# Order of the input projections around a gated scan: forget slots third and fourth, the scan's values beside its first steps

## The chip, the cores and the metric

One core of one Trainium2 chip (trn2). The metric is the device time of one execution in microseconds. TensorE (PE), VectorE (DVE), ScalarE (ACT), Pool (GpSimd) and the DMA queues run their own instruction streams and meet at semaphores. Weights are streamed from HBM by the queue of SyncE (SP).

## The reference

Two layers over 512 latent and 256 context tokens of width 1024. In each layer the input, scaled and shifted by a modulation of the conditioning vector, goes through one combined projection that is cut into fourteen column groups:

```
(qa, ka, va, qb, kb, vb, qc, ic, fcf, fcb, gc, qd, kd, vd) = _split_cols(px)
```

Four head groups use them: A windowed attention, B attention with normalised and rotated queries and keys, C a gated linear recurrence in both directions (HGRN2), D neighbourhood attention. For C, qc are the queries, ic the values, fcf and fcb the logits of the forget gates forward and backward, gc the output gate. The gate is f = lb + (1 - lb) * sigmoid(z), the key 1 - f, and the state is carried over chunks, context tokens first, then latent tokens, once in each direction. The four outputs are concatenated and projected, followed by a gated residual with layer norm, a convolutional feed-forward of width 2816 and a second residual. The context tokens are dropped after layer 0.

## The kernel before

All products are float32 made of three fp32r products (high by high, low by high, high by low), so every weight is split into a high and a low half: ScalarE writes the high half (`high_weights`, L1398), Pool the low half (`low_weights`, L2415).

The projection is done in twelve slots of 256 columns: QA, KVA, QB, KVB, QC, IC, FCF, FCB, GC, QD, KD, VD. A slot is worked off in parts: `tok` parts of two token tiles (L945), or `feat` parts of 128 features over the latent or the context tokens (L939). A part has four pieces, which `project` issues.

`ORDERS` gives the order of the slots in each layer. `mixer_jobs(l)` cuts it in two: the own stage, worked off before the scan, and the parts beside the scan, whose pieces are dealt out to the scan's units. In layer 0 the own stage also holds 21 modulation products (`mod`, L850), numbers 8 to 28, which are dealt out between the parts; each reads one weight slot of 1 MB.

The scan (`hgrn`) has 24 units per layer: forward 12 and backward 12, each direction two context tiles and four latent tiles, two head pairs per tile. In layer 1 the context units (0 to 3 and 12 to 15) have no output and only carry the state. For a unit Pool prepares the gate (`YB`, `KB`, L2381 to L2384), ScalarE takes the logarithm (L1508), VectorE scans it (L2012) and subtracts references (L2022), ScalarE takes exponentials (L1532 to L1538), VectorE forms the queries and keys (L2033, L2047), TensorE makes the score maps (L1081) or only turns the keys (L1088), VectorE copies them under a mask (L2089), and TensorE makes the output and the state (L1104 to L1115). TensorE's queue is: maps of unit i, the first piece of the unit, outputs of unit i - 1, the rest of the pieces.

After each projection part ScalarE copies the sum out of PSUM (`take_projections`). VectorE then does, in order of the parts: for a forget part `forget` (add, reciprocal, scale: L1990 to L1992), for QB and KVB `square_heads` (L1871 to L1882) and, after Pool's root (`head_roots`, L2345), `rotate` (L1901 to L1938), for QA and KVA `rotate` alone. VectorE enters the scan only when it has done this for the whole own stage. A rotation is held back by one part (`pending`), and beside the scan by one unit (`waiting`). Pool, too, takes the roots of the own stage before the first gate preparation.

Weights go through a ring of places (`ring_plan`). SP issues the loads in the order of their first use (`STREAM`), each when the slot that held the place has been used; a load that waits holds up those behind it. Places 0 to 2 are `WR`, place 3 is `U[:, 3072:5120]`, open to the first 29 modulation slots. The gates of FCB are written to `U[:, 3072:4608]` (`cz[1]`), those of FCF to `U[:, 4608:6144]` (`cz[0]`). The rule takes the free place whose slot has its last use first:

```
place = min(free, key=lambda p: -1 if holder[p] is None else final[STREAM[holder[p]]])
```

Before, layer 0's own stage was QC, GC, IC, QB, KVB, FCF, with FCB beside units -2 and -1; layer 1's was QC, GC, IC and the context half of FCF, with the rest of FCF beside units -2 and -1 and FCB beside units 0 to 3.

Of the kernel before, what the change touches and what calls it, by code (L numbers as in the profile page):

```python
# [4 lines left out]

# [1 line left out]
D_MODEL, SEQ, CTX, DEPTH = 1024, 512, 256, 2  # L7
# [3 lines left out]
NLT, NCT = SEQ // P, CTX // P  # L11
# [16 lines left out]
RING = 3  # L28
# [7 lines left out]
QA, KVA, QB, KVB, QC, IC, FCF, FCB, GC, QD, KD, VD = range(12)  # L36
# [10 lines left out]
def slot_parts(l, s):  # L47
# [4 lines left out]
    if s in FEATURE:  # L52
# [1 line left out]
    return [("tok", p, 0) for p in range(2 + ctx)]  # L54


ORDERS = ((QC, GC, IC, QB, KVB, FCF, FCB, QA, KVA, VD, QD, KD),
          (QC, GC, IC, FCF, FCB, QA, KVA, QB, KVB, VD, QD, KD))
PIECES = 4
UNITS = 4 * NT  # L60


def mixer_jobs(l):

    whole = lambda s: [(("in", l, s, 0), p) for p in slot_parts(l, s)]
    order = ORDERS[l]
    gate = order.index(FCF)
    own = [p for s in order[:gate] for p in whole(s)]
    if l == 0:
        own = own[:2] + own[4:6] + own[2:4] + own[6:]  # L70
    forget = whole(FCF)
    extra = [(("mod", n // 24, n % 24, 0), ("mod", n, 0)) for n in range(MOD_FIRST, 24 + EARLY)] if l == 0 else []
    mixed, n = own[:1], len(own) - 1
    for k, part in enumerate(own[1:]):
        mixed += [part] + extra[k * len(extra) // n:(k + 1) * len(extra) // n]
    if gate == 3:
        mixed += forget[:2]
        early, flow = forget[2:], [p for s in order[gate + 1:] for p in whole(s)]
    else:
        mixed += forget  # L80
        early, flow = whole(FCB), [p for s in order[gate + 2:] for p in whole(s)]
    span = lambda p: 5.8 if p[0] == "tok" else 2.9 if p[2] else 5.45
    total = sum(span(p) for _, p in flow)
    jobs, at = [], 0.0
    for i, (key, part) in enumerate(early):
        jobs.append((key, part, [2 * i // len(early) - 2] * PIECES))
    for key, part in flow:
        steps = [at + span(part) * q / PIECES for q in range(PIECES)]
        jobs.append((key, part, [int(t / total * (UNITS + 1)) for t in steps]))
        at += span(part)  # L90
    return mixed, jobs


def weight_splits(l):
# [62 lines left out]
def ring_plan():  # L157

    final = {key: n for n, key in enumerate(USES)}
    places = RING + 1 + ENTRANCE + 1  # L160
    holder, count, plan = [None] * places, [0] * places, []
    for n, key in enumerate(STREAM):
        kind, l = key[:2]
        first = kind == "mod" and (l == 0 or key[2] < EARLY)
        inner = kind in ("up", "down") or l > 0 and (kind == "mod" and not first or key in (("in", l, QC, 0), ("in", l, GC, 0)))
        free = range(1 if inner else 0, RING + 1 if first else RING)
        if kind == "mod" and l == 0 and key[2] < MOD_FIRST:
            free = range(SPARE - 1, 0, -1)
        if kind in ("up", "down") and l == DEPTH - 1 or kind == "mod" and l > 0 and key[2] >= LATE:
            free = (SPARE,) + tuple(free)  # L170
        place = min(free, key=lambda p: -1 if holder[p] is None else final[STREAM[holder[p]]])
        count[place] += 1
        plan.append((place, count[place], holder[place]))
        holder[place] = n
    return plan
# [6 lines left out]
def hybrid_backbone(nc, weights, x, ctx_in, consts, masks, params, bias_d, ln_rows, kept, vrows, out):  # L182
# [14 lines left out]
    with stack:  # L197
# [35 lines left out]
        whole = lambda e: (e[:, 0:2 * TOK], e[:, 2 * TOK:ENTRY])  # L233
# [173 lines left out]
        job_act = sem("job_act")  # L407
# [69 lines left out]
        jobs = []  # L477
        for l in range(DEPTH):
            own, late = mixer_jobs(l)
# [51 lines left out]
        for l in range(DEPTH):  # L531
            for d in range(2):
                order = [NLT + c for c in range(NCT)][::1 - 2 * d] + list(range(NLT))[::1 - 2 * d]
# [13 lines left out]
        beside, pieces_at = {}, {}  # L547
# [40 lines left out]
        for l in range(DEPTH):  # L588
            au = atts_of[l]
            first = n_chunk  # L590
# [99 lines left out]
        for m, (l, i) in enumerate(res):  # L690
            total = FT if i else KT
# [148 lines left out]
        def _(pe):  # L840
# [223 lines left out]
            def hgrn(l):  # L1064
# [54 lines left out]
                for i in range(len(us) + 1):  # L1119
                    if i < len(us):  # L1120
                        u = us[i]
                        pe.wait_ge(ke, u.g + 1)
                        if i >= 2:
                            if us[i - 2].out:
                                pe.wait_ge(atd, us[i - 2].no + 1)
                            if us[i - 2].state:
                                pe.wait_ge(kd_in, us[i - 2].ns + 1)
                        if u.out:
                            score_maps(u)
                        if u.state:  # L1130
                            turn_keys(u)
                    here = pieces_at[l, i]
                    ahead = int(1 <= i < len(us) and len(here) >= 2)
                    for j, q in here[:ahead]:
                        project(l, j, q)
                    if i >= 1:
                        outputs(us[i - 1])
                    for j, q in here[ahead:]:
                        project(l, j, q)
# [579 lines left out]
        def _(dve):  # L1719
            steps = [0]  # L1720
# [236 lines left out]
            def project(l):  # L1957
                pending = []
# [5 lines left out]
                for j in own_of[l]:  # L1964
# [12 lines left out]
                    if j.slot == GC:  # L1977
                        dve.wait_ge(job_act, j.after[0])
                        for i in range(2):
                            g = cg[:, 2 * j.a + i, :]  # L1980
                            dve.tensor_tensor(g, g, onorm[:, l, :], ALU.mult)
                assert not pending

            def forget(j):
                lo, hi = (0, SEQ) if j.b == 0 else (SEQ, TOK)
# [651 lines left out]
```

## Time and profile before

| | |
|---|---|
| median of 3 runs | 1959.86 us (1958.93 to 1963.39) |
| profiled execution | 1959.74 us, its span 1957.9 us |
| mean granted clock of TensorE | 0.984 |
| TensorE matmul / weight load | 1865.0 us / 1583.4 us |
| VectorE, ScalarE, Pool | 1307.4, 889.0, 929.8 us |
| DMA | 179.38 MB, mean 92 GB/s |
| layer 0: own stage, scan | about 57 to 180 us, 180 to 385 us |
| layer 1: own stage, scan | about 1177 to 1215 us, 1215 to 1426 us |

The profile is of one execution. Busy times are those of the engine's own instructions; an engine that waits is idle. The granted clock is the share of full speed that TensorE was given in a stretch: 1.00 is 2.4 GHz, 0.5 is 1.2 GHz, a mean between them says for how much of the stretch it was at the lower one.

### The profile page before, as it was taken

The numbers are of one execution on the slowest core, as the hardware profiler recorded it, in microseconds if no ns is written. First come the engines' busy times: TensorE is split into PE (matmuls) and PEld (weight loads), VectorE is DVE, ScalarE is ACT, GpSimd is POOL, SyncE is SP. The second block draws the span as 40 slices with busy tenths as digits, with TensorE's granted clock in tenths as the row PEclk, the third lists the DMA queues.
The fourth block names the chain that finished last, engine by engine and source line by source line (L and its number), as shares of the span: only waits on it lengthen the run. The fifth ranks groups of instructions, "written<-read, shape, count | busy, mean of one in ns | idle before, by whom it ended". The sixth has DMA issues, their size and how long they took to land.

```text
span 1957.9 us, 32562 instructions
## 1 busy us (share of the span) xinstructions
PE 1865.0 (95%) x12406; PEld 1583.4 (81%) x12406; DVE 1307.4 (67%) x2506; ACT 889.0 (45%) x1909; POOL 929.8 (47%) x770
## 2 busy tenths in 40 slices
PE   6899799999999999999999999998999989999997
PEld 4788798867778888888888878898877778888886
DVE  4238999676684977978735263998776858247545
ACT  3224688577533222222343343665567443333542
POOL 3135567121435344554453344666432545765743
PEclk8999899999999999999999999999999999999999
DMA  8563101220111322333222121101130313223321
GB/s 356 216 221 124 41 27 34 74 84 2 44 65 44 130 99 95 108 108 108 87 76 86 54 87 65 66 31 42 50 135 2 130 43 129 105 89 140 119 107 44
DMA packets 29545, 179.38 MB, mean 92 GB/s; under 512 B 3024, under 2 KB 6224, under 8 KB 10320
## 3 DMA queue, kind: packets, MB, share of 16 engines
q1 hardware_dynamic: 26720, 169.18, 23.8%
q10 hardware_dynamic: 2672, 8.13, 1.1%
q8 instruction: 100, 1.64, 0.3%
q14 instruction: 53, 0.43, 0.1%
HBM read 172.05 MB, written 5.24 MB: 91 GB/s over the span
## 4 chain that ended last, share of the span: by engine, by line
PE 70%; DVE 19%; issue 4%; ACT 3%; DMA 2%; POOL 2%; DVEq 0%; SPq 0%; ACTq 0%; POOLq 0%
PE PS L1342 22%; PE PS L1237 19%; PE PS L945 8%; PE PS L939 5%; DVE W L1756 4%; PE PS L1199 3%; PE PS L1175 3%; PE PS L1081 2%; PE PS L1159 2%; DMA WR<-in_weights 2%; DVE W L1754 1%; DVE U L1991 1%; PE PS L1293 1%; PE PS L1165 1%; PE PS L850 1%
## 5 line engine op out<-in xcount | busy, mean ns | idle before, releaser
L1342 PE MATMUL PS<-XH,WS 128*128 128x512 f32 x2016 | 540.3, 355 | 0.9 <-POOL WS L2482 0.9
L1342 PEld LDWEIGHTS PS<-XH,WS 128*128 128x128 f32 x2016 | 358.1, 189 | 54.4 <-POOL WS L2482 1.3
L1342 PE MATMUL PS<-XL,WS 128*128 128x512 f32 x1008 | 356.9, 354 | 0.0
L2482 POOL TENSOR_TENSOR WS<-WR,WS 128x1024 fp32r<-128x1024 f32 x78 | 189.8, 2433 | 260.0 <-ACT WS L1624 260.0
L1692 ACT ACTIVATE W<-PS,PR 128x768 f32<-128x768 f32 (+1 forms) x88 | 78.0, 886 | 416.6 <-PE PS L1342 354.4
L1342 PEld LDWEIGHTS PS<-XL,WS 128*128 128x128 f32 x1008 | 190.7, 189 | 26.3
L2304 DVE SCALAR_TENSOR_TENSOR W<-PS,PR,W 128x511 f32<-128x511 f32 (+1 forms) x132 | 82.9, 656 | 179.7 <-ACT W L1692 179.7
L2415 POOL TENSOR_TENSOR WL<-WR,EU 128x512 fp32r<-128x512 f32 x96 | 131.0, 1392 | 131.1 <-ACT EU L1398 131.1
L945 PE MATMUL PS<-EU,XH 128*128 128x256 f32 x624 | 186.8, 300 | 5.8 <-issue 5.5
L945 PE MATMUL PS<-WL,XH 128*128 128x256 f32 x624 | 179.0, 288 | 0.0
L945 PE MATMUL PS<-EU,HL 128*128 128x256 f32 x624 | 177.2, 288 | 0.0
L945 PEld LDWEIGHTS PS<-EU,XH 128*128 128x128 f32 x624 | 122.6, 197 | 13.6 <-issue 10.7
L1756 DVE SCALAR_TENSOR_TENSOR W<-WR,SC,W 128x256 f32<-128x256 f32 x210 | 130.2, 661 | 3.7
L945 PEld LDWEIGHTS PS<-WL,XH 128*128 128x128 f32 x624 | 122.9, 197 | 0.0
L945 PEld LDWEIGHTS PS<-EU,HL 128*128 128x128 f32 x624 | 121.7, 197 | 0.1
L2442 POOL COPY W<-ST 128x256 f32<-128x256 f32 x30 | 15.0, 500 | 197.9 <-DVE ST L2143 197.9
L1237 PE MATMUL PS<-XH 128*128 128x512 f32 x450 | 107.8, 390 | 0.0
L1237 PE MATMUL PS<-EW 128*128 128x512 f32 x450 | 106.5, 390 | 0.2 <-DVE W L2309 0.2
L939 PE MATMUL PS<-XH,EU 128*128 128x512 f32 (+1 forms) x288 | 102.1, 366 | 3.5 <-ACT XH L1406 3.5
L1237 PE MATMUL PS<-XL 128*128 128x512 f32 x420 | 100.1, 389 | 0.0
L1237 PE MATMUL PS<-EU 128*128 128x512 f32 x420 | 99.3, 390 | 0.0
L1237 PEld LDWEIGHTS PS<-EW 128*128 128x128 f32 x450 | 84.2, 188 | 18.1 <-DVE W L2309 0.8
(231 smaller groups left out, 4264.8 us busy)
## 6 DMA issues: line engine op xcount, KB each, us to landing
WR<-in_weights SPq DMA_DIRECT2D x115, 1024.0 KB, 4.8
U<-in_weights SPq DMA_DIRECT2D x16, 1024.0 KB, 7.6
H<-in_weights SPq DMA_DIRECT2D x13, 1024.0 KB, 4.8
H<-in_x SPq DMA_DIRECT2D x2, 2048.0 KB, 11.6
U<-in_bias SPq DMA_DIRECT2D x2, 1792.0 KB, 9.8
H<-in_ctx SPq DMA_DIRECT2D x2, 1024.0 KB, 16.1
U<-in_ln_rows ACTq DMA_DIRECT2D x2, 1024.0 KB, 5.4
WR<-in_weights SPq DMA_DIRECT2D x4, 512.0 KB, 3.6
```

Source lines behind the costliest of these rows:

```text
L939: return pe.matmul(bank(j.bank, CTX if j.b else SEQ), w[:, j.a * P:(j.a + 1) * P], acts, start=start, stop=stop)
L945: return pe.matmul(bank(j.bank)[:, i * 256:(i + 1) * 256], acts, w, start=start, stop=stop)
L1081: mm = pe.matmul(maps_of(u, hh)[:, m * 64:(m + 1) * 64], KE[par][rows, m, :], later(QL[par][rows, m, :], u, w), start=True, stop=True)
L1175: mm = pe.transpose(tb[:, (b - c.lo) * P:(b - c.lo + 1) * P], PB[c.a.r % 2][:, b * P:(b + 1) * P], ident)
L1199: mm = pe.matmul(bank(7)[64 * hh:64 * hh + 64, a.p * P:(a.p + 1) * P], vv[a.grp][:, kt, vc:vc + 64], PT[a.r % 2][:, b * P:(b + 1) * P], st ...
L1237: mm = pe.matmul(bank((job + 4) % 8), acts[a][:, t * P:(t + 1) * P], rows[b], start=(q.k == 0 and n == 0), stop=(q.k == total - 1 and n == 2))
L1342: mm = pe.matmul(PS[u.pos][:, lo:hi], w[:, part, k, :], src[:, k, lo:hi], start=(k == 0 and src is xh3 and part == 0), stop=(k == KT - 1 a ...
L1692: act.activation(dst[:, 0:n], PS[u.pos][:, 0:n], ACT.Identity, bias=convp[:, l, 3, jj:jj + 1], scale=convp[:, l, 1, jj:jj + 1]).then_inc(b ...
L1756: ins = dve.scalar_tensor_tensor(acc, wk[:, k, :], scv[:, k, v:v + 1], acc, ALU.mult, ALU.add)
L2304: ins = dve.scalar_tensor_tensor(y[:, lo + 1:hi], ps[:, lo:hi - 1], convp[:, l, 0, jj:jj + 1], y[:, lo + 1:hi], ALU.mult, ALU.add)
L2415: pool.tensor_tensor(raw_piece(WL, l, at, q), raw_piece(WR, l, at, q), high_piece(l, at, q), ALU.subtract).then_inc(in_low, 1)
L2482: pool.tensor_tensor(ws5[:, u.c % 2, 1], half_slot(u), ws5[:, u.c % 2, 0], ALU.subtract).then_inc(w_low, 1)
```

## The change

In both layers the slots FCF and FCB come third and fourth, and all of FCF and FCB belongs to the own stage. IC follows beside units -2 and -1. In layer 0 the rest of the order is as before; in layer 1 the order beside the scan is QB, QA, KVA, KVB, VD, QD, KD. The pieces beside layer 1's scan are dealt out by a share: 1.75 for a unit without output (0 to 3 and 12 to 15), 1 for the others. Place 3 of the ring is open only to modulation slots that are used before FCF in layer 0. TensorE waits for ScalarE's copies of IC before the outputs of unit 0, and VectorE does the last held-back rotation at the end of its own stage.

```diff
-ORDERS = ((QC, GC, IC, QB, KVB, FCF, FCB, QA, KVA, VD, QD, KD),
-          (QC, GC, IC, FCF, FCB, QA, KVA, QB, KVB, VD, QD, KD))
+ORDERS = ((QC, GC, FCF, FCB, QB, KVB, IC, QA, KVA, VD, QD, KD),
+          (QC, GC, FCF, FCB, IC, QB, QA, KVA, KVB, VD, QD, KD))
...
-    gate = order.index(FCF)
+    gate = order.index(IC)
     own = [p for s in order[:gate] for p in whole(s)]
     if l == 0:
         own = own[:2] + own[4:6] + own[2:4] + own[6:]
-    forget = whole(FCF)
+    early, flow = whole(IC), [p for s in order[gate + 1:] for p in whole(s)]
     extra = [(("mod", n // 24, n % 24, 0), ("mod", n, 0)) for n in range(MOD_FIRST, 24 + EARLY)] if l == 0 else []
-    mixed, n = own[:1], len(own) - 1
+    mixed, n = own[:1], len(own) - 2
     for k, part in enumerate(own[1:]):
         mixed += [part] + extra[k * len(extra) // n:(k + 1) * len(extra) // n]
-    if gate == 3:
-        mixed += forget[:2]
-        early, flow = forget[2:], [p for s in order[gate + 1:] for p in whole(s)]
-    else:
-        mixed += forget
-        early, flow = whole(FCB), [p for s in order[gate + 2:] for p in whole(s)]
     span = lambda p: 5.8 if p[0] == "tok" else 2.9 if p[2] else 5.45
     total = sum(span(p) for _, p in flow)
+    share = [1.75 if l + 1 == DEPTH and i % (UNITS // 2) < 2 * NCT and i < UNITS else 1.0 for i in range(UNITS + 1)]
+    ends = [e / sum(share) * total for e in itertools.accumulate(share)]
...
-        jobs.append((key, part, [int(t / total * (UNITS + 1)) for t in steps]))
+        jobs.append((key, part, [sum(e <= t + 1e-6 for e in ends) for t in steps]))
...
+def ahead_of_gates():
+
+    own = [key for key, _ in mixer_jobs(0)[0]]
+    return own[:own.index(("in", 0, FCF, 0))]
...
+    opening = ahead_of_gates()
...
-        free = range(1 if inner else 0, RING + 1 if first else RING)
+        free = range(1 if inner else 0, RING + 1 if first and key in opening else RING)
...
+                    if i == 1:
+                        pe.wait_ge(job_act, beside[l, -1][-1].after[0])
...
-                assert not pending
+                if pending:
+                    rotate(pending.pop())
```

## Rows read from the trace of the kernel before

**Rows 1.** The page: busy time of each engine.

```profile
PE 1865.0 (95%) x12406; PEld 1583.4 (81%) x12406; DVE 1307.4 (67%) x2506; ACT 889.0 (45%) x1909; POOL 929.8 (47%) x770
```

**Rows 2.** Windows: length; busy (count) of PE, PEld, DVE, ACT, POOL; clock, DMA share, GB/s.

```profile
57.00:90.00 33.00, 27.02 (x251) 22.02 (x244) 9.35 (x33) 10.50 (x25) 7.25 (x7) 0.90 0.60 224
90.00:182.00 92.00, 91.87 (x824) 80.78 (x823) 47.74 (x139) 27.23 (x57) 35.21 (x36) 1.00 0.55 198
...
196.30:225.50 29.20, 19.98 (x186) 19.25 (x186) 28.68 (x45) 15.34 (x51) 12.51 (x19) 0.82 0.11 38
225.50:300.00 74.50, 71.12 (x747) 68.62 (x745) 73.29 (x190) 59.04 (x190) 49.99 (x69) 1.00 0.10 34
...
1209.00:1252.80 43.80, 40.86 (x235) 35.20 (x233) 36.21 (x45) 23.52 (x63) 30.22 (x44) 0.96 0.21 73
1252.80:1320.70 67.90, 65.34 (x657) 63.42 (x656) 63.21 (x147) 44.10 (x139) 43.81 (x56) 1.00 0.10 34
1320.70:1354.70 34.00, 26.62 (x195) 25.38 (x194) 30.29 (x84) 17.01 (x52) 23.96 (x32) 0.90 0.17 60
```

**Rows 3.** TensorE's waits, from 57 to 90, 182 to 400 and 1209 to 1430.

```profile
PE PS L850 <- DMA U<-in_weights: 4.9, 1, 4.9
...
PE PS L1081 <- DVE W L2047: 12.3, 6, 7.6
...
PE PS L1088 <- DVE W L2047: 5.1, 2, 3.9
...
PE PS L945 <- issue: 2.8, 1, 2.8
```

**Rows 4.** The chain that ended last, layer 0's own stage: start, length, what.

```profile
70.91 3.09 PE PS L939 x24
...
74.01 7.41 DMA WR<-in_weights
...
81.56 1.94 PE PS L850 x16
83.50 6.43 PE PS L945 x48
...
168.46 5.49 PE PS L939 x24
```

**Rows 5.** DMA issues from 121 to 129.7: count, KB, time to landing.

```profile
WR<-in_weights SPq DMA_DIRECT2D x1, 1024.0 KB, 4.8
U<-in_weights SPq DMA_DIRECT2D x1, 1024.0 KB, 7.2
```

**Rows 6.** VectorE, groups of 182 to 218, then its timeline there.

```profile
L1991 DVE RECIPROCAL U<-U 128x512 f32<-128x512 f32 (+1 forms) x5 | 13.6, 2713 | 0.2
...
L1992 DVE TENSOR_SCALAR U<-U,SC 128x512 f32<-128x512 f32 (+1 forms) x5 | 3.6, 714 | 0.2
...
185.66 1.50 DVE L2012 TENSOR_TENSOR_SCAN W<-W 128x128 f32<-128x128 f32 x1
...
192.89 1.09 DVE L2033 TENSOR_TENSOR W<-W,U 128x896 f32<-128x896 f32 x1 [2.50 <-ACT W L1538]
```

**Rows 7.** The last KVB part in the chain, and Pool's root after it.

```profile
153.18 5.95 PE PS L945 x48
...
164.08 1.36 POOL L2345 TENSOR_TENSOR ST<-ST,SC 128x2 f32<-128x2 f32 x2 [4.85 <-DVE ST L1879]
```

**Rows 8.** VectorE: reciprocals of 1209 to 1262.2; rotations, layers 1 and 0.

```profile
L1991 DVE RECIPROCAL U<-U 128x256 f32<-128x256 f32 (+1 forms) x8 | 20.4, 2553 | 0.3
...
1324.02 0.85 DVE L1901 TENSOR_TENSOR U<-U,ST 128x256 f32<-128x256 f32 x2
...
1329.62 0.76 DVE L1938 TENSOR_TENSOR U<-U 128x256 f32<-128x256 f32 x2
...
1275.94 2.64 DVE L1932 TENSOR_TENSOR U<-U,CN 128x128 f32<-128x128 f32 x2
...
244.57 0.49 DVE L1932 TENSOR_TENSOR U<-U,CN 128x128 f32<-128x128 f32 x2
```

More of the change, by code:

```diff
@@ L2 @@
 from concourse import mybir
+import itertools
 from contextlib import ExitStack
```

## The prediction

> **What bounds the kernel now.** I read the page first: TensorE is busy for 95% of the span [rows 1], so a reordering can only give back TensorE's idle time and the time it runs at the lower clock. Then I cut both layers into stretches, reading TensorE's busy time, VectorE's busy time and the granted clock [rows 2], and asked in each stretch what TensorE waited for [rows 3].
>
> Layer 0. From 57 to 90 us TensorE is idle for 6.0 us at a mean clock of 0.90: weight loads are late. From 90 to 182 us it is idle for 0.1 us. From 196.3 to 225.5 it is idle for 9.2 us at clock 0.82, with VectorE busy for 28.7 of 29.2 us; the longest single wait is one of 7.6 us of the score maps for VectorE [rows 3]. From 225.5 to 300 VectorE is busy 98% and TensorE 95%: the two run almost even.
> Layer 1. From 1209 to 1252.8 TensorE is idle 2.9 us, to 1320.7 (units 4 to 11, the forward units with outputs) 2.6 us with VectorE at 93%, and to 1354.7 (units 12 to 15, no outputs) 7.4 us at clock 0.90.
> So about 12 us of layer 1 and 16 us of layer 0 are idle time, a few more are half clock, and both engines sit near their limit elsewhere.
>
> **The change, layer 0, up to the scan.** The order goes from IC, QB, KVB, FCF to FCF, FCB, QB, KVB, and IC moves beside units -2 and -1, where FCB was. Nothing is added or taken out: IC is three parts of 5.95 us [rows 7], 17.85 us, and FCB two of 5.5 and two of 3.1 [rows 4], less the overlap of one part with the next an estimated 16.8 us. The own stage is thus 1.05 us shorter and the scan's start 1.05 us longer.
> The ring is where it costs. Place 3 lies in U at 3072 to 5119, which is where the gates of FCB and FCF begin. Once they are written early, only what is used before FCF may go there. I walked the planner's rule over the new order: FCF sits in place 1, FCB in place 2, and the modulation slots 13 to 17 all follow each other in place 0; then 18 to 28 all follow each other in place 1. Before, they alternated between two places. A load can only be issued when the slot before it in that place is used, so each modulation product waits for a whole load less the projection that lies between.
> Prices: a lone load lands after 4.8 us; the second of two issued 1.2 us apart after 7.2 [rows 5] (7.4 in [rows 4]); a modulation product takes 1.0 (half of the 1.94 at the low clock), a long part 5.5 to 5.95, a context part 3.1 [rows 4, 7].
> Walking it: slot 12 (behind a 3.1 us part) waits 1.5; slot 14, its load second behind FCB's, 7.2 - 3.1 - 0.25 = 3.85; slot 15 behind a context part 1.5; slot 16 and 17 nothing; slot 18 comes right after 17 and takes the place of FCF: 4.8 - 1.2 = 3.6; slots 19 and 20 1.6 each; 21, 22 nothing; 23, second behind KVB's load, 0.9; 26, second behind IC's, 0.3; 28, directly behind 27 in the same place, 4.8 + 0.1 = 4.9. Sum 19.75. The old waits of this stage go: 4.9 for slot 13, whose issue was held on SP's queue behind IC's (74.01, 7.41 us for slot 14 behind it [rows 4]), and 1.1 for others, in all 6.0 [rows 2, 3], and 3.0 of low clock after the long one (the products of slots 13 and 14 at half pace, 1.94 for one, and 6.43 for a part that takes 5.95 [rows 4, 7], with the start of the load behind them). Slot 12's new 1.5 stands in their place. Net 19.75 - 9.0 - 1.05 = +9.7; I take 8.1, because 1.6 of these waits fall where the clock drop below stretches the projection in front of them.
> The clock: the rows show it at its lower level (1.2 of 2.4 GHz) after idle times of 4.9 and 7.6 us (mean 0.90 and 0.82 over their stretches [rows 2, 3]). The new waits of 3.85, 3.6 and 4.9 are of that size. The last has nothing behind it to absorb it, 3.0; the first two feed the next wait and cost an estimated 0.7 together: +3.7. Bounds 0 and 9.
> So the own stage ends at about 179.7 + 11.8 = 191.5.
>
> **The scan's start.** Removed from VectorE: four forgets of FCB after units -2 to 0. Their reciprocals are 13.6 less FCF's last 3.35, 10.2 us, and with the two scalar instructions around each (0.71 mean for the second, some 0.4 for the first [rows 6]) 13.9. All lay on the path: this is the stretch with VectorE at 98%. The cover that they find is the own stage, where VectorE is busy 47.7 of 92 us [rows 2].
> Added in front: KVB is now the last own part, so its square, Pool's root (1.36 us, [rows 7]) and Pool's first gate preparation come after it, and VectorE's pending rotation. By the rows the root ended 6.3 after TensorE's last product of that part (159.1 to 165.4 [rows 7]); with two modulation sums ahead of it 0.8 more, the preparation and a logarithm 2.6: the first scan starts at 9.7 after the stage's end, where it was 6.0 (185.66 against 179.7 [rows 6]). ScalarE takes both IC parts before the first exponentials, which ends them 2.1 later than the 7.2 they took (185.66 to 192.89). VectorE's path: 11.8 + 3.7 + 2.1 - 13.9 = +3.7. TensorE's path: after IC's 18 us it waits about 3 us for the first maps, then reaches unit 2 at 34.2 after the stage's end; before, 38.4 and 3.7 lost to the clock. 11.8 - 7.9 = +3.9, less some 3 of the later waits for VectorE, which now has a lead. Layer 0: +3.5. The added wait of TensorE for IC's copies stands at unit 1, behind it the outputs of unit 0; the copies are 10 us old by then: 0.
>
> **Layer 1.** FCF and FCB go first; eight forgets (reciprocals 20.4 us, with their neighbours 31 [rows 8]) begin under the own stage at 1193 and end at about 1230. The ring is not touched: no load of place 3 there. TensorE's order becomes IC until 1242.4, then QB over units 0 and 1, QA over 1 to 3, by the share of 1.75. Units 0 to 3 and 12 to 15 get 5.8 to 7.25 us of projection, units 4 to 11 get 26.1 where they had 39.2. QA's low parts (four of Pool's 1.4 us) are split one unit ahead: a wait of about 1 us in place of today's 2.8 [rows 3].
> VectorE decides units 4 to 11. From 1209 to 1320.7 it is busy 36.2 + 63.2 = 99.4 us [rows 2]; less 31 of forgets 68.4. QB's two square-and-rotate groups now come before unit 12: from 1324.02 to 1330.38 one rotation is 6.4 us [rows 8], with the square 7.9, twice 15.8, and KVB's first square 1.3: 85.5. Some 4 of it can be done before QB's first part lands at 1249, VectorE takes it up at 1252.9 and waits 3 for the state sums: 1252.9 + 81.5 + 3 = 1337. TensorE alone could be at unit 12 at 1324. From there before took 34.0 + 71.3; less 8.9 of projections already done, 7.4 of idle time, 3.0 of low clock, plus 1 for small waits: 87.0, end 1424.0 against 1426.1. Layer 1: -2.1. Bounds: 13 less when VectorE does not bind, 8 more when its work all meets Pool's.
> Here the trace shows the same kind of rotation instruction at two prices: 2.64 us for two beside Pool's work and 0.49 alone in layer 0 [rows 8]; I took the mixed sums. The Trainium skill (GPSIMD Engine Reference, Specifications) says that GpSimd's SBUF interfaces are shared with VectorE where VectorE has two SBUF inputs. By that rule alone every rotation beside a split pays the high price and layer 1 ends at +4; the mixed rows give -2.
> Another sentence by itself: the Trainium skill (DMA: Bandwidth & Descriptors, Anatomy of one DMA) puts a load at about 2.0 us and its bytes at 436 GB/s, 4.4 us for a megabyte; by it the six lone waits shrink by 0.4 each and the time would be some 2.4 us lower, while the rows say 4.8.
>
> **Sum.** +3.5 - 2.1 = +1.4 us. The profiled execution took 1959.74 us with a span of 1957.9; the median shown is 1959.86. 1961.3 predicted, span 1959.3. A difference under 0.2% (3.9 us) is about what this kernel's measurement can't tell from none.
>
> **Rivals.**
> 1. The clock falls after most of the new waits of layer 0, also the 1.5 us ones. For: the waits come every 4 to 6 us from slot 14 to 20. Against: waits of this length during the scans leave the mean clock at 1.00 [rows 2]. Price 5 more: 1966.5. It ends slower; it decides from 2.5 us of extra half clock. Chance 0.22.
> 2. VectorE does not bind units 4 to 11: its lead from the early forgets and fewer collisions with Pool let it keep up. For: TensorE then has 13 us less to do there, and units 12 to 15 lose their 7.4 us. Against: the 85.5 us above. Half of the 13 us: 1961.3 - 8 = 1953.5. Faster. Chance 0.32.
> 3. The change does not do what it says in layer 0: the first scan waits for KVB's chain and ScalarE's copies, and the 13.9 us are only waited for elsewhere, TensorE idle again at the first maps with a clock drop. Price 6 to 8: 1968.5. Chance 0.13.
> Forecast, no measurable change, 0.33; its own range 1957 to 1964.
> Range for 8 in 10: 1950, a little beyond rival 2, to 1970, beyond rival 3. Faster 0.32, same 0.33, slower 0.35.
>
> **What would show it.** TensorE idle in the own stage of layer 0 with weight loads as releaser, six or more waits of 1.5 to 5 us, and a stage end near 191; one lone wait of 4.9 before the last KVB part. No wait of 7.6 for VectorE at the third unit; first maps near 212.7. In layer 1 no low clock and hardly any idle time in units 12 to 15, but 10 us or more of idle time in units 4 to 11 with VectorE above 95%. The prediction is wrong when layer 0's stage ends before 186 or after 197, or when TensorE stays busy in units 4 to 11 of layer 1.

## The result, and the profile after

The changed kernel takes 1974.13 us (median of 6 runs, 1970.07 to 1976.22); the kernel before, beside it, 1960.12 us (6 runs). The ratio is 1.0053, its 95% interval 1.0037 to 1.0069. The ratio is not the quotient of these two medians, which would be 1.0071: the medians are 14.0 us apart, the ratio stands for 10.4 us, and the ratio with its interval is what is used below. So the kernel is slower by about half a per cent, where 1961.3 and no measurable change were forecast. The profiled execution took 1976.22 us with a span of 1974.4, the longest of its six runs, so the profile's difference of 16.5 us in span is more than the ratio's 10.4 us, and part of that is explained at the end of this section.

The page of the profile says that the amount of work is the same: 12406 matmuls in both. They took TensorE 1865.0 us before [rows 1] and take 8 us more now, at a mean clock of 0.981 where it was 0.984.

```profile
PE 1873.2 (95%) x12406; PEld 1588.4 (80%) x12406; DVE 1307.2 (66%) x2506; ACT 890.8 (45%) x1909; POOL 929.4 (47%) x770
```

The windows of layer 0 (length; busy and count of PE, PEld, DVE, ACT, POOL; clock, DMA share, GB/s):

```profile
57.00:90.00 33.00, 27.15 (x254) 23.44 (x256) 13.16 (x38) 13.50 (x26) 10.81 (x10) 0.97 0.54 192
90.00:182.00 92.00, 82.46 (x656) 68.45 (x650) 49.98 (x100) 18.93 (x41) 22.45 (x20) 0.95 0.51 184
...
200.00:240.00 40.00, 38.03 (x373) 36.93 (x373) 31.00 (x65) 30.38 (x94) 33.97 (x45) 1.00 0.08 28
240.00:300.00 60.00, 55.15 (x574) 53.11 (x573) 59.24 (x155) 46.80 (x151) 39.70 (x55) 1.00 0.10 37
```

From 90 to 182 us TensorE was busy for all but 0.1 us [rows 2]; now it is idle for 9.5 us, at clock 0.95. The start of the scan, idle for 9.2 us of 29.2 at clock 0.82 before [rows 2], is now idle for 2.0 us of 40, at clock 1.00. TensorE's waits, first those from 57 to 215 us:

```profile
PE PS L854 <- DMA WR<-in_weights: 18.6, 7, 4.8
PE PS L854 <- DMA U<-in_weights: 1.7, 1, 1.7
```

L854 is the modulation product (L850 before). The chain of the changed kernel (start, length, what) shows where these waits stand and what comes with them:

```profile
73.12 1.07 PE PS L854 x16
...
81.42 7.28 DMA WR<-in_weights
...
88.83 1.94 PE PS L854 x16
90.77 4.97 PE PS L943 x24
...
95.96 1.00 PE PS L854 x16
...
109.55 4.90 DMA WR<-in_weights
...
114.59 1.10 PE PS L854 x16
115.69 0.02 issue
115.71 7.09 DMA WR<-in_weights
...
122.94 1.10 PE PS L854 x16
124.04 0.02 issue
124.06 4.72 DMA WR<-in_weights
```

Four pieces of this chain are loads of one megabyte. The one of 4.72 us was alone, and the one of 7.28 was issued 1.25 us behind another. The one of 4.90 had another issued 1.25 us behind it, which took 6.15 us, and the one of 7.09 was issued 1.24 us before that one landed. Each is issued 0.02 us after the product or part that freed its place, and TensorE stands until it has landed. Behind the wait that ends at 88.83 the product takes 1.94 in place of 1.00 us and the context part 4.97 in place of about 3.1 [rows 4]: the lower clock. The same at the last wait of the stage, for slot 28, 4.84 us long, in TensorE's timeline (start, length, what, idle time before it):

```profile
181.32 1.07 PE L854 MATMUL PS<-WR,W 128*32 128x256 f32 x16
187.23 1.93 PE L854 MATMUL PS<-WR,W 128*32 128x256 f32 x16 [4.84 <-DMA WR<-in_weights]
```

The stage ends at 195.8 us, 16.1 later than before (179.7). The first scan on VectorE starts at 205.13, the first maps at 217.37. The rest of layer 0 has no long wait: these are TensorE's from 205 to 400 us.

```profile
PE PS L1085 <- DVE W L2054: 4.8, 5, 1.7
PE PS L1108 <- ACT W L1564: 3.5, 4, 1.6
```

The single wait of 7.6 us in [rows 3] is gone. Attention in layer 0 starts at 394.9 where it started at 384.6, 10.3 us later, and layer 1 starts 10.5 us later. Layer 1's scan, in windows:

```profile
1284.30:1347.70 63.40, 57.13 (x550) 55.23 (x550) 57.12 (x153) 43.91 (x139) 38.55 (x57) 0.92 0.06 18
1347.70:1375.30 27.60, 27.60 (x229) 26.84 (x228) 20.57 (x75) 15.71 (x50) 17.25 (x27) 1.00 0.14 49
1375.30:1397.00 21.70, 19.79 (x120) 16.81 (x120) 14.42 (x26) 13.91 (x45) 15.56 (x18) 0.69 0.17 61
```

and its waits from 1215 to 1445 us:

```profile
PE PS L1085 <- DVE W L2054: 9.4, 4, 3.7
PE PS L943 <- issue: 1.9, 1, 1.9
```

Units 4 to 7 wait for VectorE. Units 12 to 15 (the second window) are now full at clock 1.00, where 34.0 us held 26.62 busy before [rows 2]. Then comes one wait of 1.9 us ahead of QD's first piece, for the low halves of its weights, which Pool makes in 6.89 us from 1374.36, and behind it a stretch at clock 0.69. Layer 1's attention starts at 1442.8 where it started at 1426.4: 16.4 later, 10.5 of it layer 0's, so 5.9 is layer 1's.

These 5.9 us are not a fixed price. Four kernels here have the same program for the scan of layer 1, and it (first turned keys to attention) took 190.2 us in the changed kernel, 190.3 in the one with TensorE kept busy, 187.2 in the one with layer 1 alone and 184.0 in the one with a second place, at clocks 0.94, 0.94, 0.95 and 0.97. There is one profile of each, so whether it differs between executions of one kernel or between kernels is not shown. The mean clock of the whole, which was taken in each run, does differ between the six runs of the changed kernel, from 0.981 to 0.984, and the two longest have 0.981.

### The profile page after: what moved, and what is told of

Read it like the earlier page. It is cut to its first block, busy times and chain, and to the rows that moved or that the text cites. A ratio compares the mean times of both kernels' runs of the same rounds, so it can differ in the third digit from the quotient of the medians.

```text
span 1974.4 us, 32562 instructions
## 1 busy us (share of the span) xinstructions
PE 1873.2 (95%) x12406; PEld 1588.4 (80%) x12406; DVE 1307.2 (66%) x2506; ACT 890.8 (45%) x1909; POOL 929.4 (47%) x770
## 4 chain that ended last, share of the span: by engine, by line
PE 70%; DVE 18%; issue 4%; DMA 3%; ACT 2%; POOL 2%; DVEq 0%; SPq 0%; ACTq 0%; POOLq 0%
PE PS L1348 22%; PE PS L1243 19%; PE PS L943 7%; PE PS L949 7%; DVE W L1762 4%; DMA WR<-in_weights 3%; PE PS L1205 3%; PE PS L1181 3%; PE PS L1085 2%; PE PS L1165 2%; DVE W L1760 1%; PE PS L1171 1%; PE PS L1299 1%; PE PS L854 1%; DVE W L2054 1%
## 5 line engine op out<-in xcount | busy, mean ns | idle before, releaser
L2311 DVE SCALAR_TENSOR_TENSOR W<-PS,PR,W 128x511 f32<-128x511 f32 (+1 forms) x132 | 82.9, 656 | 179.7 <-ACT W L1698 179.7
L943 PE MATMUL PS<-HL,EU 128*128 128x512 f32 (+1 forms) x288 | 98.4, 357 | 1.3 <-DVE HL L1802 1.1
## 6 DMA issues: line engine op xcount, KB each, us to landing
H<-in_ctx SPq DMA_DIRECT2D x2, 1024.0 KB, 16.4
```

The lines of the kernel that those rows point to most:

```text
L943: return pe.matmul(bank(j.bank, CTX if j.b else SEQ), w[:, j.a * P:(j.a + 1) * P], acts, start=start, stop=stop)
L2311: ins = dve.scalar_tensor_tensor(y[:, lo + 1:hi], ps[:, lo:hi - 1], convp[:, l, 0, jj:jj + 1], y[:, lo + 1:hi], ALU.mult, ALU.add)
```

## The experiments

Twelve kernels ran, in three batches, each beside runs of the kernel before in the same batch. Ratios are to that kernel; where a difference in us is said to be by the ratios, it is worked out from them. A difference of two ratios from different batches is less certain than their intervals say, since the kernel before itself had medians of 1961.40, 1964.89 and 1961.55 in the three.

### First batch: which layer, and what in layer 0

**Layer 0 alone.** Layer 0 as in the change, layer 1 as before.

```diff
 def mixer_jobs(l):
+    if l != 0:
+        return jobs_before(l)
...
-          (QC, GC, FCF, FCB, IC, QB, QA, KVA, KVB, VD, QD, KD))
+          (QC, GC, IC, FCF, FCB, QA, KVA, QB, KVB, VD, QD, KD))
```

> Layer 0 as in the change, layer 1 as before. Theory 1 (most of the loss is layer 0's own stage, where the modulation slots follow each other in one place of the ring): the span grows by 10.4 us, as the first products of layer 1 came 10.5 us later in the profile after, so a ratio near 1.005. Rival (the loss is layer 1's, by the way its pieces are dealt out; layer 0's waits are covered by the shorter scan): at most +4 us, ratio under 1.002.

Measured: 1971.81 us (10 runs), ratio 1.0043 (1.0027 to 1.0058). By the ratio that is 8.4 us of the changed kernel's 10.4. Waits for loads are 17.5 and 1.7 us, and attention in layer 0 starts at 393.2.

**Layer 1 alone.** Layer 1 as in the change; layer 0 and the ring as before.

```diff
 def mixer_jobs(l):
+    if l != 1:
+        return jobs_before(l)
...
-        free = range(1 if inner else 0, RING + 1 if first and key in opening else RING)
+        free = range(1 if inner else 0, RING + 1 if first else RING)
```

> Layer 1 as in the change, layer 0 and its ring as before. Theory 1: layer 1's part by the profile after is 5.9 us, of which a low clock of 13.7 us length explains some 6, which need not come in every execution: +0 to +6 us, ratio 1.000 to 1.003. Rival (layer 1 carries the loss): +10 us or more, ratio 1.005.

Measured: 1962.65 us (12 runs), ratio 1.0001 (0.9988 to 1.0014). Layer 0 carries the loss; layer 1's part neither gains nor loses, within 2.7 us to either side.

**Place 3 closed in the kernel before.** Only the ring changes, in the way the change needs it.

```diff
-        free = range(1 if inner else 0, RING + 1 if first else RING)
+        free = range(1 if inner else 0, RING + 1 if first and l == 0 and key[2] < 13 else RING)
```

> The kernel before with one thing changed: place 3 of the ring is closed to the modulation slots 13 to 28, as the change had to do, with every order as before. By the planner's rule slots 13 to 27 then all use place 0 and four of them (14, 18, 21, 25) stand directly behind their forerunner in the same place. Theory 1: each waits for a whole load, 4 x 4.9 us, and the clock drops behind them, some 2 us each: +20 to +28 us. Rival (loads are prefetched well enough and the waits seen after are another thing's): under +4 us.

Measured: 1996.43 us (4 runs), ratio 1.0168 (1.0145 to 1.019), so 33 us. Its chain, its window, against 91.87 us busy in [rows 2], and its waits for loads from 57 to 215 us:

```profile
95.08 7.31 DMA WR<-in_weights
...
110.83 4.65 DMA WR<-in_weights
...
115.62 1.93 PE PS L850 x16
117.55 6.83 PE PS L945 x48
```

```profile
90.00:182.00 92.00, 73.78 (x649) 63.29 (x649) 26.65 (x90) 17.58 (x37) 22.84 (x20) 0.89 0.46 165
```

```profile
PE PS L850 <- DMA WR<-in_weights: 33.2, 10, 5.1
```

The closed place does harm by itself, without any new order, and in the old order three times what the change costs. It did more than expected, because six waits of 4.6 to 5.1 us came where four had been counted, and after each of the six the product and the part behind it ran at the lower clock (1.93, and 6.83 for a part of 5.95).

**A second place for the modulation slots.** The changed kernel, with 2048 further columns of U, free until the gates, for slots from 12 on.

```diff
+EXTRA = SPARE + 1
...
+        if first and (l > 0 or key[2] > MOD_FIRST + 3):
+            free = tuple(free) + (EXTRA,)
...
-                  + [H[:, NLT * D_MODEL:NT * D_MODEL]])
+                  + [H[:, NLT * D_MODEL:NT * D_MODEL], U[:, 7680:7680 + SLOT]])
...
+                elif place == EXTRA:
+                    sp.wait_ge(xl_pool, POOL_K)
+                    sp.wait_ge(xl_dve, KT - POOL_K)
```

> The kernel after, with one more place for the modulation slots from number 12 on, in U[:, 7680:9728], which lies idle from the split of the activations to the scan. Theory 1: the 20.2 us of waits for weight loads in layer 0's own stage and the 5.8 us of low clock behind them go, but for a wait or two; own stage ends near 171 instead of 195.8, the time falls by 20 to 25 us against after and by 6 to 14 against before. Rival (the forgets or the DMA bandwidth would bound the stage anyway): the stage ends after 185 and the time stays above before's.

Measured: 1952.16 us (6 runs), ratio 0.9942 (0.992 to 0.9964), 22 us under the changed kernel. Its window:

```profile
90.00:182.00 92.00, 87.86 (x737) 74.77 (x736) 58.19 (x141) 21.43 (x44) 27.39 (x27) 1.00 0.53 195
```

The count of products rises from 656 to 737 at clock 1.00. The 92 us reach beyond the stage, which now ends at about 173.7; what is left of the load waits is one of 3.2 us and one of 0.6, beside one of 0.5 for VectorE. With its loads fed, the stage is 22 us shorter than the changed kernel's 195.8: the waits and the clock behind them had made it long. The sum agrees: 20.2 us of waits less the 4.3 that are left, and 5.8 for the lower clock (worked out below), are 21.7.

### Second batch: the kernel before fed as well, and layer 1's parts

**The kernel before with the further place.** The same edit on the kernel before.

> The kernel before with the further place for modulation slots, every order as before. It shows how much of second_place's gain is the ring alone. Theory 1 (the order itself is worth the scan's earlier start, 5.8 us in the profile after): the ring alone gives back at most the waits of 6.0 us and 3.0 us of low clock of the early own stage, -4 to -9 us, and second_place stays some 5 us below it. Rival (the order is worth nothing, all is ring): as low as second_place, 1952.

Measured: 1955.04 us (6 runs), ratio 0.9951 (0.9935 to 0.9967). By the ratio that is 9.6 us less than the kernel before, a little more than the theory's 4 to 9, and the second place with the new order of layer 0, in the next experiment, is by the ratios only 1 us below it. Most of what the further place gives against the kernel before is thus not the change's: the kernel before takes it too.

**The second place, layer 1 as before.** The kernel with the second place, with the edit of the first experiment.

> second_place with layer 1 as before the change. Theory 1 (layer 1's part of the change is neutral: VectorE binds units 4 to 11 as much as it relieves 12 to 15): 1952 +- 2, no difference to second_place. Rival (layer 1's part loses the 5.9 us of the profile after): 1946 to 1948.

Measured: 1953.92 us (6 runs), ratio 0.9945 (0.9928 to 0.9961), as in the theory: with the share of 1.75, layer 1's part makes no difference that could be measured (0.9942 with it, in another batch).

**The second place, all shares 1.0.**

```diff
-    share = [1.75 if l + 1 == DEPTH and i % (UNITS // 2) < 2 * NCT and i < UNITS else 1.0 for i in range(UNITS + 1)]
+    share = [1.0 if l + 1 == DEPTH and i % (UNITS // 2) < 2 * NCT and i < UNITS else 1.0 for i in range(UNITS + 1)]
```

> second_place with the share of 1.75 replaced by 1.0: layer 1's pieces dealt out evenly, the order kept. Theory 1 (with 1.75, QB's and QA's rotations come so early and so close that VectorE is behind when the output units begin; TensorE idles about 9 us in units 4 to 11): evenly dealt, TensorE's idle time there falls under 4 us, but units 12 to 15 starve as before; time within 3 us of second_place. Rival (the 1.75 is what helps in layer 1): 4 us or more slower.

Measured: 1944.95 us (6 runs), ratio 0.9903 (0.9884 to 0.9922). Both the theory and its rival fell: it is 7 us faster than with 1.75, and the fastest kernel here. But not all of the 7 us is the share's. At layer 1's attention the two profiles are 7.9 us apart, and 4.4 of them arise before layer 1's scan, where both kernels run the same instructions; the scan's part is 3.5.

**The second place, QA and KVA ahead of QB and KVB in layer 1.**

```diff
-          (QC, GC, FCF, FCB, IC, QB, QA, KVA, KVB, VD, QD, KD))
+          (QC, GC, FCF, FCB, IC, QA, KVA, QB, KVB, VD, QD, KD))
```

> second_place with QA and KVA ahead of QB and KVB in layer 1, the share kept. Theory 1 (QB's two square-and-rotate groups of 7.9 us each hold VectorE back at the start): QA's cheaper rotations stand in units 0 to 3, but QB's come into the output units 4 to 9, where VectorE has no room: TensorE idles more than 9 us there, 0 to +4 us. Rival (it is the order QB first that costs): -3 us or more.

Measured: 1950.89 us (6 runs), ratio 0.9929 (0.9913 to 0.9945). That is 2.5 us less than with QB first by ratios of two batches, between the theory's 0 to +4 and the rival's -3, and not clear of the noise. Layer 1's scan took 184.9 us, against 184.0 with QB first: no gain there.

### Third batch: the share, the order of layer 0, the clock

**The changed kernel with the share at 1.0.** The one-line edit above, without the further place.

> The changed kernel with one number set back: layer 1's context units 4 to 7 and 12 to 15 get the same share of projection work as the others (1.0 in place of 1.75); the order of layer 0 and everything else stays. Theory (the number alone costs time in layer 1: 1944.95 against 1952.16 us where only it differed, in kernels with a further weight place): here too 6 to 8 us less than the changed kernel's 1974, so 1966 to 1968 us, a ratio to the kernel before of about 1.0015; layer 1 from its attention of layer 0 to its own attention shorter by 4 to 10 us, with no wait of 1.9 us ahead of QD's first piece. Rival: the gain came only together with the further place, which brings layer 1 in earlier: then within 3 us of 1974, ratio 1.004 to 1.007.

Measured: 1967.84 us (10 runs), ratio 1.003 (1.0019 to 1.0042). By the ratios that is 4.5 us less than the changed kernel, under the 6 to 8 expected, though the median lies in the range. (The units of the share are 0 to 3 and 12 to 15, as the diff has it; the expectation misnames the first four.) Layer 1's scan (first keys to attention) in four kernels, one window of each; the changed kernel's:

```profile
1252.60:1442.80 190.20, 176.85 (x1509) 164.89 (x1508) 142.32 (x367) 113.54 (x352) 104.69 (x140) 0.94 0.12 43
```

the same with the share at 1.0:

```profile
1253.90:1434.50 180.60, 170.55 (x1511) 159.50 (x1510) 145.65 (x367) 113.17 (x352) 108.93 (x140) 0.97 0.13 45
```

with the second place, share 1.75:

```profile
1233.20:1417.20 184.00, 170.46 (x1511) 159.35 (x1510) 142.87 (x367) 113.11 (x352) 105.12 (x140) 0.97 0.13 44
```

and with the second place, share 1.0:

```profile
1228.80:1409.30 180.50, 170.17 (x1511) 159.11 (x1510) 145.56 (x367) 113.15 (x352) 109.19 (x140) 0.97 0.13 45
```

At equal clock the share of 1.75 costs 3.5 us, 3.2 of them idle time (13.54 against 10.33). The waits say where. From 1200 to 1445 us those of the score maps for VectorE are, with the second place, at 1.75 and at 1.0:

```profile
PE PS L1091 <- DVE W L2060: 9.6, 4, 3.6
```

```profile
PE PS L1091 <- DVE W L2060: 8.8, 6, 3.7
```

So an equal share leaves the waits for VectorE almost as they were; what goes is the 1.9 us ahead of QD's first piece and one wait of 0.5. The other 6.2 us of the changed kernel's scan are clock: idle time is 13.35 us there and 13.54 with the second place, and TensorE's busy time for the same products is 176.85 against 170.46.

**The second place, share 0.75.**

```diff
-    share = [1.0 if l + 1 == DEPTH and i % (UNITS // 2) < 2 * NCT and i < UNITS else 1.0 for i in range(UNITS + 1)]
+    share = [0.75 if l + 1 == DEPTH and i % (UNITS // 2) < 2 * NCT and i < UNITS else 1.0 for i in range(UNITS + 1)]
```

> The kernel with the further weight place, and 0.75 as the share of layer 1's context units (1.0 gave 1944.95 us, 1.75 gave 1952.16). Theory (the share of 1.0 keeps both kinds of unit fed; with less the context units run out of projection work and TensorE waits for VectorE in units 4 to 7 and 12 to 15, while the other units are bound by TensorE): 1947 to 1953 us, a ratio of 0.991 to 0.994, worse than at 1.0 by 2 to 8 us. Rival (the fewer pieces beside the outputs the better, over this stretch of the scale as well): 1940 to 1944 us, a ratio of 0.988 to 0.990. A second rival: nothing changes within 2 us, and what the share of 1.75 cost was the late QD piece and its low clock alone.

Measured: 1950.8 us (5 runs), ratio 0.9943 (0.993 to 0.9956). The time is in the range of the first theory, but its mechanism is not what the trace shows: most of the waiting is not for VectorE in the context units. From 1200 to 1445 us the profile has, as its two largest groups of waits,

```profile
PE PS L955 <- issue: 5.3, 2, 4.0
PE PS L1125 <- ACT W L1562: 2.0, 1, 2.0
```

The 4.0 us end at 1275.17, just after Pool has made the low halves for that piece (L2428, 1272.51 to 1275.07): with more pieces in the units with outputs, projections come before Pool has their weights. The scan took 181.6 us against 180.5. At layer 1's attention the two profiles are 4.7 us apart, and 3.7 of them arise before layer 1's scan, where both kernels run the same instructions. So the time fell into the range by luck in the main, and that 1.0 is better than 0.75 is not shown beyond this 1.1 us of one profile each.

**Layer 0 as before with the further place, layer 1 new with share 1.0.**

> Layer 0 in the order of the kernel before, with the further weight place; layer 1 in the changed order with a share of 1.0. It differs from the kernel of 1944.95 us in layer 0's order alone. Theory (with its loads fed, the new order of layer 0 reaches the attention 5 to 6 us sooner by the profile): 1947 to 1951 us, a ratio of 0.991 to 0.994, so 2 to 6 us longer than with the new order. Rival (layer 0's order is worth nothing even when it is fed, as 0.9945 against 0.9951 with layer 1 as before hinted): 1943 to 1947 us, a ratio of 0.989 to 0.991.

Measured: 1951.43 us (5 runs), ratio 0.9948 (0.9935 to 0.9961). Its waits from 57 to 215 us:

```profile
PE PS L1123 <- DVE W L2092: 8.9, 2, 7.6
PE PS L892 <- DMA U<-in_weights: 3.0, 2, 2.0
```

The wait of 7.6 us for VectorE is that of [rows 3], which the new order of layer 0 takes away. Attention in layer 0 starts at 379.7 here and in the kernel before with the further place, against 372.2 to 376.9 in the five kernels with the new order and the second place: once its loads are fed, the new order is ahead at that point in every profile. How much it is worth in time is less sure: 0.45% with the new layer 1 (0.9948 to 0.9903, across batches), 0.06% with the old one (0.9951 to 0.9945, in one batch). The profile with the old one is that of 376.9: TensorE's clock was 0.96 there from 90 to 182 us, where the other four, with the same instructions, start attention at 372.2 to 373.9.

**The changed kernel, with TensorE kept busy in three waits.** The transposes of the identity go into a scratch bank; nothing reads them.

```diff
                         pe.wait_ge(mod_done, n - 3)
+                        for _ in range({14: 15, 18: 16, 28: 20}.get(n, 0)):
+                            pe.transpose(bank(6)[:, 0:P], ident, ident)
                         mod_products(n, j.key)
```

> The changed kernel, and in the waits for the modulation slots 14, 18 and 28 TensorE issues 15, 16 and 20 transposes of the identity into a scratch bank, so that it does not stand idle there; no result uses them. It measures the clock's part of the loss by itself. Theory (the three stretches at the low clock that follow these waits, of 6.9, 3.4 and 3.4 us, cost 5.8 us of the own stage): the granted clock between 90 and 200 us rises from about 0.94 to near 1, the loads land when they did, and the time falls by 2 to 5 us to 1969 to 1972 us, a ratio of 1.003 to 1.0045; 1.7 us come back as waits for slot 15. Rival (the waits for the loads set the pace, and a faster clock only makes the next wait longer): the low stretches are gone, but the own stage ends within 1 us of 195.8 and the time is within 1.5 us of 1974.

Measured: 1970.61 us (6 runs), ratio 1.0052 (1.0033 to 1.007), the changed kernel's 1.0053. Its chain:

```profile
80.93 6.91 DMA WR<-in_weights
87.84 0.04 issue
87.89 1.11 PE PS L854 x16
89.00 0.02 issue
89.02 6.13 DMA WR<-in_weights
95.15 0.14 issue
95.28 1.07 PE PS L854 x16
...
108.95 7.45 DMA WR<-in_weights
116.40 0.04 issue
116.44 1.07 PE PS L854 x16
117.52 4.54 PE PS L943 x24
```

After the first wait the clock stays up (product 1.11, not 1.94), and the context part ends early; then TensorE stands for slot 15's load until 95.28, where the changed kernel, with its slow part, started that product at 95.96 and had not waited. Nothing was gained on the way: from slot 14's product to slot 15's it took 7.39 us here and 7.13 there. But the loads were not the same. The load for slot 15 was issued 1.8 us sooner and took longer, here and then in the changed kernel:

```profile
WR<-in_weights SPq DMA_DIRECT2D x1, 1024.0 KB, 6.1
```

```profile
WR<-in_weights SPq DMA_DIRECT2D x1, 1024.0 KB, 4.9
```

At slot 18 the load takes 7.45 us, where it took 4.90, with another load issued 1.25 us behind it in both kernels; that product starts at 116.44, 1.85 later than in the changed kernel. Why these two loads took longer is not shown. The stage ends at 197.5, not sooner.

The fill did not do what it was for, either. It cured only one low stretch of the three (the others have 4.54 for a context part, and 1.89 for slot 28's product), a new one stands from 175.4 us, and the clock from 90 to 200 us is 0.95 in both kernels. So it doesn't measure the term of the clock. Neither account is settled by it: the rival's no gain in time was met, but its bound on the stage's end was missed by 0.7 us and its low stretches are not gone, and the 3.8 us by which two loads were longer are enough to hide what the theory expected. The times alone could not have told a gain of 2 us from none: the medians are 3.5 us apart, the ratios are equal, and each has an interval of 3.5 us to either side.

## Why the prediction was wrong

What held. The new load waits of layer 0 were named and priced: 20.2 us of gaps from 57 to 196 us against 19.75; slot 28's was 4.84 for 4.9, slot 14's 4.19 for 3.85, slot 18's 3.85 for 3.6, slots 19 and 20 2.31 and 1.63 for 1.6 each. The lone load of slot 20 took 4.72 us, near the 4.8 of the rows. The Trainium skill (DMA: Bandwidth & Descriptors, Anatomy of one DMA) gives its figures for loads that GpSimd issues, and these come from SyncE; the estimate of 4.4 us that follows from them is too short here, and the trace decides for the rows. The first scan came 9.3 us after the stage's end (9.7 forecast), the first maps 21.6 (21.2), unit 2 at 34.0 (34.2). In layer 0's own stage the clock fell after the three waits for which it was forecast and after none of the shorter ones (2.31 us and less), so rival 1's account fell there, though its sign was right. Rival 3 fell too; there was no clock drop at the first maps.

In layer 1 unit 12 came at 1347.7 less layer 0's 10.5, so 1337.2 (1337 forecast), with VectorE as the releaser of 9.4 us in units 4 to 7: rival 2 fell. That the time was met to 0.2 us is partly luck, since VectorE was busy for 90% of units 4 to 11 and not for over 95%, and TensorE's clock was 0.92 there, which the forecast had not.

Three of the prediction's sums don't come out as written. The 13.9 us taken off VectorE would be 14.6 by the means beside it; by VectorE's timeline it is 14.0. Rival 2's 1961.3 less 8 is 1953.3 and not 1953.5, and half of 13 is 6.5. For layer 0 the two paths give +3.7 and +3.9 and the second has 3 more to be taken off, but +3.5 is written; step 3 below comes back to this.

What failed is the size of the terms below, all on the same side, and most of all those of layer 0's own stage. By the runs, layer 0 costs 8.4 us (ratio 1.0043) where +3.5 was forecast, and layer 1 0.2 us (1.0001) where -2.1 was. The sizes below are those of one profile, the longest of six runs, and are larger.

1. **"I take 8.1"**: 1.6 us of waits were deducted from the 9.7 because a slow projection would hide them. Slot 15's wait, forecast at 1.5, was indeed hidden, but the others were 2.0 us longer than forecast, so the gaps that were left still add up to 20.2 us against 19.75. +1.6, and +0.5 for the waits themselves.
2. **"+3.7" for the clock in layer 0.** Three stretches at the lower level, seen in the products and parts from 88.8, 115.6 and 187.2 us on, cost 5.8 us by the lengths of their products and parts: 2.8 and 1.5 for the first two, where 0.7 was taken for both because the next wait would absorb them, and 1.5 for the last, where 3.0 was taken. +2.1. The own stage ends at +16.1 and not +11.8 by these two steps. What the clock would give back by itself, with the loads left as they are, is not shown by the run with transposes. The sum of both terms is what the stage loses, and the second place shows that sum: 22 us against a stage that is fed.
3. **"Less some 3 of the later waits for VectorE, which now has a lead."** Up to unit 2 the forecast held (step 2's excess aside), but from there to the attention 4.1 us were to be gained (from +7.6 to +3.5), by the missing low clock and the lead, and 1.4 were gained (165.05 us where it took 166.46). The low clock was gone, and TensorE's busy time there fell by 2.8 us where 3.7 had been put. The waits for VectorE grew. Before, from 219 to 385 us, behind the long one, they were

```profile
PE PS L1081 <- DVE W L2047: 3.4, 4, 1.4
```

and now they are 4.8 in five. VectorE was busy 59.24 of 60 us from 240 to 300, 99%, against 98% from 225.5 to 300 before [rows 2], so no lead reached them: +2.7 with the smaller gain of the clock. These three make layer 0 +10.5 where +3.5 was forecast.
4. **"Plus 1 for small waits" in layer 1, and no term for the clock.** From unit 12 on 87.0 us were forecast and 95.1 measured; in the kernels with the second place and with layer 1 alone the same stretch took 88.9. The wait for QD's low halves was 1.9, and behind it came 21.7 us at clock 0.69. The same 21.7 us of layer 1's program, with the same wait, in the kernel with the second place had

```profile
1355.90:1377.60 21.70, 19.80 (x177) 17.11 (x176) 19.41 (x37) 17.46 (x54) 18.02 (x22) 1.00 0.17 62
```

that is, 177 matmuls in 19.80 us of busy time, against 120 in 19.79. It is the clock, and it did not come each time: of the four profiles with this wait two have clock 0.69 behind it (the changed kernel and the one with TensorE kept busy) and two 1.00 (the second place and layer 1 alone). The whole scan differed by 6.2 us for it, most of the 8.1. What decides between the two is not shown.
5. **The share.** The forecast took the dealing by 1.75 as a gain: context units full, no idle time there. They are full, but QD's first piece then waits for Pool; the waits of units 4 to 7 for VectorE (9.4 us) are hardly less with an equal share (8.8 against 9.6 with the second place). An equal share costs less by 3.5 us of the scan, and by 4.5 us of time in the changed kernel (1.003 against 1.0053). No other share had been compared with it. This is not a further part of the sum: its waits are in the 8.1 and in unit 12's time already.

Together: 4.3 (the own stage), 2.7 and 8.1 are 15.1, against the 16.4 - 1.4 = 15.0 us by which the sum missed the profile. The sum had a term for the clock where the longest waits are, and none for what the short waits of layer 1 can set off.

What stays open: how large the clock's term is when it is alone, since no run here took away all its stretches with the loads left as they were; and why the new order of layer 0 is worth 0.45% in one pair of kernels and nothing in the other, beyond the clock of one profile. Layer 1's stretches at the low level vary between profiles of the same program (clock 0.94 to 0.97 for one and the same scan), and one profile for each kernel doesn't average them.

## What to carry to other kernels

When a reordering moves a buffer's first write earlier, count first which loads lose that buffer: here the closing of one place in a ring of four cost more than the new order gave, and by itself in the old order it cost 33 us. Price the waits for loads first, each as the time of the load less the work that lies between its issue and its need, and don't deduct from them an overlap with a slow stretch that is itself an estimate; here the deduction of 1.6 us was eaten up by waits that were longer than forecast. And if work is dealt out to steps that have slack, time the equal deal too, because the steps that it is taken from may not be the ones that were short of TensorE.

## What the runs showed of the hardware

- A wait of 1.9 us was followed by 13 us or so at 1.2 GHz in two profiles and by none in two others, with the same instructions around it (clock 0.69 against 1.00 over 21.7 us). In the kernel with transposes, waits of 2.10 and 3.05 us left the clock up, and one of 2.52 us, behind a fill of 2.40, did not.
- The first of two loads of one megabyte isn't always quick: with another issued 1.25 us behind it, it took 4.90 us in one kernel and 7.45 in another. In the kernel with transposes two loads with no other of their queue in flight took 6.1 us, where most such loads took 4.6 to 4.9.
